# A hybrid decoder trunk on one core: the experts' weight pipeline is recut

## The reference

```python
def swiglu(h, w_gate_up, w_down):
    g, u = jnp.split(h @ w_gate_up, 2, axis=-1)
    return (jax.nn.silu(g) * u) @ w_down

def moe_ffn(h, router, w_gate_up, w_down):
    ...
    top_v, top_i = lax.top_k(logits, TOP_K)            # 2 of 8
    gates = jax.nn.softmax(top_v, axis=-1)
    combine = jnp.sum(jax.nn.one_hot(top_i, N_EXPERTS) * gates[..., None], axis=1)
    for e in range(N_EXPERTS):
        out = out + combine[:, e:e + 1] * swiglu(t, w_gate_up[e], w_down[e])
```

## Time and profile before

| | |
|---|---|
| median of 3 runs | 1663.63 us (1662.83 to 1664.7) |
| span of the profiled execution | 1657.2 us |
| PE busy | 1585.0 us, 96% |
| DVE busy | 1014.2 us, 61% |
| ACT busy | 913.3 us, 55% |
| POOL busy | 971.8 us, 59% |
| read from HBM | 428.91 MB |

### The profile page before, as it was taken

The page is one execution under the profiler, slowest core; times in us unless marked ns, Lnnn a source line. Parts: engine busy times, 40 slices in busy tenths (PEclk is TensorE's granted clock), DMA queues, the critical chain, the costliest instruction groups (busy, mean ns, idle before and its releaser), DMA issues.

```text
span 1657.2 us, 22184 instructions
## 1 busy us (share of the span) xinstructions
PE 1585.0 (96%) x6965; PEld 1232.3 (74%) x6965; DVE 1014.2 (61%) x951; ACT 913.3 (55%) x904; POOL 971.8 (59%) x457
## 2 busy tenths in 40 slices
PE   7997899999888789999999999999999999999998
PEld 4666478888755656887887888888888788888886
DVE  2103344444324336778778777877877877877875
ACT  2202244443315214776776776776776776776774
POOL 1100134445211012996996896897897797797795
PEclk9997999999988888999999999999999999999999
DMA  6342255554233044999999999999999999999993
GB/s 218 114 150 79 97 187 198 177 194 161 95 132 102 0 153 159 366 367 314 364 356 323 366 367 312 365 367 312 365 364 315 364 366 312 366 366 320 358 365 139
DMA packets 322107, 430.67 MB, mean 260 GB/s; under 512 B 13878, under 2 KB 282235, under 8 KB 322044
## 3 DMA queue, kind: packets, MB, share of 16 engines
q1 hardware_dynamic: 322044, 430.01, 76.0%
HBM read 428.91 MB, written 1.05 MB: 259 GB/s over the span
## 4 chain that ended last, share of the span: by engine, by line
PE 45%; POOL 35%; issue 14%; DVE 2%; ACT 2%; POOLq 1%; DMA 1%; DVEq 0%; SPq 0%; ACTq 0%
POOL wlo L532 34%; PE PS L1012 9%; PE PS L1014 9%; PE PS L1013 9%; PE PS L863 7%; PE PS L905 3%; PE PS L831 2%; PE PS L942 2%; PE PS L1124 1%; POOLq L529 1%; PE PS L874 1%; ACT xn L666 0%; PE PS L932 0%; POOL rstd L500 0%; PE PS L1149 0%
## 5 line engine op out<-in xcount | busy, mean ns | idle before, releaser
L532 POOL TENSOR_TENSOR wlo<-ring,whi 128x384 fp32r<-128x384 f32 x378 | 945.2, 2515 | 399.5 <-ACT whi L612 394.0
L1298 DVE TENSOR_TENSOR wlo<-ring,whi 128x1664 fp32r<-128x1664 f32 x378 | 767.8, 2034 | 269.3 <-ACT whi L612 268.6
L612 ACT ACTIVATE whi<-ring 128x2048 fp32r<-128x2048 f32 x378 | 723.5, 1915 | 136.3 <-PE PS L1014 109.8
L1012 PE MATMUL PS<-whi,xhi 128*128 128x512 f32 x1120 | 449.8, 402 | 5.1 <-DVE xlo L1645 2.4
L1014 PE MATMUL PS<-whi,xlo 128*128 128x512 f32 x1120 | 438.2, 391 | 0.0
L1013 PE MATMUL PS<-wlo,xhi 128*128 128x512 f32 x1120 | 437.6, 391 | 0.0
L1012 PEld LDWEIGHTS PS<-whi,xhi 128*128 128x128 f32 x1120 | 211.0, 188 | 52.9 <-POOL wlo L532 8.9
L1014 PEld LDWEIGHTS PS<-whi,xlo 128*128 128x128 f32 x1120 | 210.7, 188 | 45.3
L1013 PEld LDWEIGHTS PS<-wlo,xhi 128*128 128x128 f32 x1120 | 211.5, 189 | 40.3
L1012 PE MATMUL PS<-whi,hhi 128*128 128x512 f32 x560 | 223.8, 400 | 1.5 <-DVE hlo L1325 1.5
L1014 PE MATMUL PS<-whi,hlo 128*128 128x512 f32 x560 | 218.7, 391 | 0.0
(11 more groups left out here) (242 smaller groups left out, 952.4 us busy)
## 6 DMA issues: line engine op xcount, KB each, us to landing
ring<-in_moe_w_gate_up SPq DMA_DIRECT2D x448, 512.0 KB, 5.3
ring<-in_moe_w_down SPq DMA_DIRECT2D x224, 512.0 KB, 5.0
ring<-in_dense_w_gate_up SPq DMA_DIRECT2D x56, 512.0 KB, 4.6
ring<-in_dense_w_down SPq DMA_DIRECT2D x28, 512.0 KB, 4.3
ring<-in_a_w_in SPq DMA_DIRECT2D x6, 1536.0 KB, 6.6
ring<-in_mem_w_kv SPq DMA_DIRECT2D x2, 2048.0 KB, 10.8
ring<-in_a_w_out SPq DMA_DIRECT2D x2, 2048.0 KB, 7.8
ring<-in_b_w_out SPq DMA_DIRECT2D x2, 2048.0 KB, 8.0
```

Of the source, the lines that this page charges most:

```text
L532: pool.tensor_tensor(wlo[:, n % CUTS, m:SLOT], ring[:, h * SLOT + m:(h + 1) * SLOT], whi[:, n % CUTS, m:SLOT].bitcast(F32), ALU.subtract). ...
L612: nc.scalar.activation(whi[:, n % CUTS, :], ring[:, h * SLOT:(h + 1) * SLOT], ACT.Copy).then_inc(S("highs"), 1)
L1012: mm(out_, lhsT=xh, rhs=wh, start=first, stop=False)
L1298: v.tensor_tensor(wlo[:, n % CUTS, 0:m], ring[:, h * SLOT:h * SLOT + m], whi[:, n % CUTS, 0:m].bitcast(F32), ALU.subtract).then_inc(S("low ...
```

## The change

The experts get their own code; the dense layer keeps the old blocks.

- **Blocks of 512.** An expert has 7 blocks (`NBE`) of 512 hidden columns. A block is six items: four gate-up items of two 128-row groups each (512 gate and 512 up columns, pieces of 2 KB), and two down items. There are still 42 items of 1 MB in an expert, with the same products, and the same six slots and three buffers. Gate and up halves now have a PSUM bank each. All seven blocks are written out; only the loop over experts remains.
- **No drain between experts.** The down items of an expert's last block come inside the first block of the next expert. Those of the last expert stand alone at the end.
- **Combine.** Its first half is issued after the gate-up items of the second block, its second half after those of the third; expert 0 has none, and the zeros are gone. The gathering of the next tokens is in the sixth block.
- **Lower halves.** DVE subtracts all 2048 columns, in the dense layer too. POOL does none.
- **Order in an item.** The eight products with `whi` come first, and wait only for ACT's part; the four with `wlo` come last.

The core of the diff, new code only, in the order of the engines:

```diff
+def expert_item(i, b, q):
+    return 6 * b + q - (0 if b == 0 and isinstance(i, int) else 2)
...
+def expert_parts(gu, dn, b, q):
+    if q < 4:
+        return [(cols(gu, g * FF + b * EB, g * FF + (b + 1) * EB)[:, 2 * q:2 * q + 2, :], slice(0, 2),
+                 slice(g * EB, (g + 1) * EB)) for g in range(2)]
...
 # ScalarE
+def expert_hi(i, b, q):
+    m, h, j = expert_slot(i, b, q)
+    if m >= CUTS or not isinstance(i, int):
+        act.wait_ge(S("through"), upto(i, PERE, NS + m - CUTS + 1))
+    act.wait_ge(S(f"slot_full{h}"), ...)
+    nc.scalar.activation(whi[:, j, :], ring[...], ACT.Copy).then_inc(S("highs"), 1)
+def expert(i):
+    first = isinstance(i, int)
+    for b in range(NBE):
+        if b == 0 and not first:
+            expert_hi(i, 0, 0)
+            expert_hi(i, 0, 1)
+        if b > 0 or not first:
+            expert_hi(i, b, 2)
+            hidden_high(i * NBE + (NB + b))
+        expert_hi(i, b, 3)
+        if b > 0 or not first:
+            expert_hi(i, b, 4)
+            expert_hi(i, b, 5)
+        if b == 1 and not first:
+            y_high()
+        act.wait_ge(S("through"), upto(i, PERE, NS + expert_item(i, b, 3) + 1))
+        nc.scalar.activation(silE, PS[0:CAP, 0, :], ACT.Silu).then_inc(S("silu"), 1)
+        if b < NBE - 1:
+            expert_hi(i, b + 1, 0)
+            expert_hi(i, b + 1, 1)
+    x_high(i + 1)
...
 # TensorE
+def expert_cut(i, b, q, j, parts):
+    pe.wait_ge(S("highs"), upto(i, PERE, PER + m + 1))
+    for out_, xh, xl, c0, first, end in parts:
+        mm(out_, lhsT=xh, rhs=whi[:, j, c0:c0 + HD], start=first, stop=False)
+        mm(out_, lhsT=xl, rhs=whi[:, j, c0:c0 + HD], start=False, stop=False)
+    pe.wait_ge(S("lows"), upto(i, PERE, PER + m + 1))
+    for out_, xh, xl, c0, first, end in parts:
+        last = mm(out_, lhsT=xh, rhs=wlo[:, j, c0:c0 + HD], start=False, stop=end)
+    last.then_inc(S("through"), 1)
+def expert(i):
+    first = isinstance(i, int)
+    pe.wait_ge(S("xlo_ready"), i + 1)
+    for b in range(NBE):
+        expert_gate_up(i, b)
+        if not first and b == 1:
+            combine(0, 6, i)          # waits for y_low and G_ready
+        if not first and b == 2:
+            pe.wait_ge(S("added0"), i)
+            combine(1, 6, i)
+        if b == 4:
+            turn_gates()
+        if b == 5:
+            pe.wait_ge(S("dispatch"), i + 2)
+            ...
+            gather()
+        if b > 0:
+            pe.wait_ge(S("h_low"), i * NBE + (NB + b))
+            expert_down(i, b, b - 1)
+        elif not first:
+            pe.wait_ge(S("h_low"), i * NBE + NB)
+            expert_down(i, 0, NBE - 1)
+        turn_expert(i * NBE + (NB + b + 1))
...
 # VectorE, within expert(i), block b
+    if b > 0 or not first:
+        expert_lo(i, b, 4)
+        expert_lo(i, b, 5)
+    if b == 1 and not first:
+        y_low(i)
+    dve.wait_ge(S("silu"), i * NBE + (NB + b + 1))
+    v.tensor_tensor(hnE, PS[0:CAP, 1, :], silE, ALU.mult).then_inc(S("h_ready"), 1)
+    if b in (1, 2) and not first:
+        add(i, f"added{b - 1}", b - 1, 6)
+    if b == 4:
+        next_dispatch(i)
+    if b < NBE - 1:
+        expert_lo(i, b + 1, 0)
+        expert_lo(i, b + 1, 1)
+ ...
+gathered(i + 1)
```

More of the change, by code:

```diff
@@ L95, in build @@
     assert NB % 2 == 0 and PER % SLOTS == 0 and PER % CUTS == 0 and len(FFN) == PER
+    EB = 4 * P
+    NBE = FF // EB
+    PERE = 6 * NBE
+    assert PERE == PER and PERE % SLOTS == 0 and PERE % CUTS == 0
+    def expert_item(i, b, q):
[4 more added lines that the diff above has]
+                     slice(g * EB, (g + 1) * EB)) for g in range(2)]
+        f = 4 * b + 2 * (q - 4)
+        return [(rows(dn)[:, f + kk:f + kk + 1, :], slice(kk, kk + 1), slice(0, D)) for kk in range(2)]
     def gu_item(b):
@@ L446, in _ @@
                     fill_big(place[n], view)
[L448 to L458, removed]
@@ L461, in _ @@
[L461 to L469, removed]
@@ L612, in hi_of, with block @@
                 nc.scalar.activation(whi[:, n % CUTS, :], ring[:, h * SLOT:(h + 1) * SLOT], ACT.Copy).then_inc(S("highs"), 1)
-            def block(i, b, nt, r=None):
+            def block(b, r=None):
                 for n in cut_item(b):
[L617 to L626, removed]
+                    if b > 0:
+                        hi_of(n, r)
+                act.wait_ge(S("through"), count(r, 3, FFN0 + gu_item(b) + 2))
+                for t in range(NT):
+                    last = nc.scalar.activation(sil[:, t], PS[:, t, 0:FB], ACT.Silu, scale=rx[:, t:t + 1])
@@ L1239, in _ @@
                 expert(i)
-            pe.wait_ge(S("xlo_ready"), passes * NE + 1)
-            combine(passes * NE)
+            pe.wait_ge(S("h_low"), passes * (NE * NBE) + NB)
+            for q in (4, 5):
+                m = q - 6
+                j, M = m % CUTS, passes * (NE * PERE) + (PER + m + 1)
+                pe.wait_ge(S("highs"), M)
+                pe.wait_ge(S("lows"), M)
+                for kk in range(2):
+                    for hh in range(2):
+                        c, c0 = 2 * (q - 4) + kk, kk * D + hh * HD
+                        last = three(PS[0:CAP, 4 + hh, :], hhiE[:, c, :], hloE[:, c, :], whi[:, j, c0:c0 + HD], wlo[:, j, c0:c0 + HD],
+                                     False, c == 3)
+                last.then_inc(S("through"), 1)
+            pe.wait_ge(S("silu"), passes * (NE * NBE) + NB)
+            for t, bank in enumerate((6, 0)):
+                combine(t, bank, passes * NE)
         @block.vector
@@ new lines, in dense, with expert_lo @@
+            def dense():
+                for b in (0, 1):
+                    block(b)
+                with dve.Fori(0, len(REST)) as r:
+                    for b in (2, 3):
+                        block(b, r)
+                for b in (NB - 2, NB - 1):
+                    block(b)
+            def expert_lo(i, b, q):
+                m, h, j = expert_slot(i, b, q)
+                dve.wait_ge(S("highs"), upto(i, PERE, PER + m + 1))
+                v.tensor_tensor(wlo[:, j, :], ring[:, h * SLOT:(h + 1) * SLOT], whi[:, j, :].bitcast(F32),
+                                ALU.subtract).then_inc(S("lows"), 1)
```

424 lines of the change are left out of this document (211 added, 213 removed).

## The result

| | median of the runs, us | lowest to highest | runs |
|---|---|---|---|
| before | 1663.22 | 1661.42 to 1664.7 | 5 |
| changed | 1673.14 | 1668.75 to 1677.0 | 5 |

The changed kernel takes 1.0066 times the time of before, interval 1.0049 to 1.0084: slower, by 9.9 us of the median. That is less than 1%, and the interval lies clear of 1. The forecast was 1679, 15.3 us more on the span. Every run's time is its span plus 1.7 to 2.1 us; the profiled execution took 1673.83 us for a span of 1672.0.

What follows compares the result with a forecast made beforehand. TensorE's own products were taken to set the pace. Experts 1 to 7 +5.0, clock +7.7, expert 0 -0.75, end +3.3 +1.0, start -0.9: span +15.3 to 1672.5, plus 6.4 makes 1679; own range 1667 to 1687, overall 1650 to 1690.

Steps and rivals of the forecast that it cites:

- The combine's wait: Second block of experts 1 to 7: TensorE waits for y_low, 3.02 us, 3.05 with restart; bounds 2.5 and 3.5.
- The removed stalls: TensorE in each expert: all 2.33 us of stalls go, giving 124.3 us per expert.
- The clock: After each combine stall, often some 3 us at half clock: 1.1 us per stall, 7.7 us in all.
- The start: Ahead of the first gather: the four zeroing products go, so it starts 0.9 us earlier.
- The end: Last two down items stand alone behind the last transposes: TensorE waits, +3.3 us, plus 1.0 us of clock.
- Expert 0: First expert: loses its stalls (-1.75) and empty combine (-1.95), gains waits around its first SiLU (+2.95): -0.75 us.
- Span to median: Whole run: the median 1663.63 us lies 6.4 above the page's span, so 6.4 us was added to the forecast span.
- The combine wasn't hidden: Rival at the combine: stalls go and y_low is ready when TensorE comes, 29 us less, 1650 us; chance 14%.
- It did not cancel: Rival on the total: stall without clock loss and slightly larger removed stalls cancel, 1665 us; chance 10%.
- TensorE waited for no loop's code: Rival at the expert loop's head: ScalarE's or VectorE's longer loop pauses, 3.2 us more per expert, 1701 us; chance 8%.
- The rival's own model, SyncE's pause: SyncE's 5.3 us gap after branching back to its expert loop's head, taken as what ScalarE's or VectorE's loop might pay.

Runs made afterwards that it cites:

- early-output: Changed kernel with y_high moved right behind the third item's cut and y_low behind the hidden lower half, in the second block; 1648.09 us, ratio 0.992.
- half the bytes: Kernel before, loading only half of each weight item for experts 1 to 7; 1663.55 us, ratio 1.0002.
- the kernel with GpSimd's share back: Changed kernel with output early and end and expert 0 mended, but GpSimd subtracting 384 of 2048 columns in the experts; 1645.9 us, ratio 0.9896.
- VectorE alone: Kernel before with all 2048 columns of every lower half on VectorE, GpSimd's share and its waits gone; 1652.17 us, ratio 0.9935.

## Why the prediction was right, and where it was off

The mechanism was right, and so was the size of its main term: the combine lost its cover, seven times, behind the chain cut, lower half, y_low. The early-output experiment takes away just that and turns 0.7% slower into 0.8% faster. The total was forecast half too high, 15.3 us where 9.9 were measured. Term by term, on the span:

- **The combine's wait**, forecast 3.02 us and 3.05 with the restart, measured 2.98, and 3.06 with the restart by the early-output kernel's expert. VectorE's 2048 columns, forecast 2.3, take 2.29.
- **The removed stalls**, forecast 2.33 us per expert, measured 2.71. Most of the other 0.38 is the pitch in the experts: I took the gain there at 0, with 0.4 us as its upper bound. Between products without a wait the mean distance went from 0.2280 to 0.2274 us, 0.3 us over an expert's some 500 products. Freer transfers, the condition that I set for it, don't look like the cause: with half the bytes an expert kept its 126.68 us. An expert without the wait takes 123.91, not 124.3. Together the wait and the stalls make +1.9 us where I had +5.0.
- **The clock, the term that was mis-sized most**: forecast 7 x 1.1 = 7.7 us, measured 2 x 1.64 = 3.3. I took the share of idles followed by the lower clock from places among light work (six of seven); among the experts' dense products it is two of seven. The price of one, forecast 1.5, was close. With the two terms above this makes experts 1 to 7 +5.2 us where I had +12.7. The first profile's two falls were met again in the two later ones; what decides which idles are followed stays open.
- **The start**, forecast -0.9 us, measured +1.3. TensorE does reach the gather 0.84 us sooner (8.67 us from 622.88 to 631.55, against 9.51 from 617.94 to 627.45). But I costed the zeroing products only as work, and they had also been cover: without them TensorE idles for 2.66 us, the low clock goes on, and the gather takes 2.10 us more. So the sign of this term was wrong.
- **The end**, forecast +3.3 and 1.0: the idle is 2.85 us, and from the final combine's first product to the end it is 8.03 us against 6.83, +1.2 from the clock. VectorE's order is what ends the idle:

```profile
1652.93 0.60 ACT L641 ACTIVATE hhi<-PS 128x512 fp32r<-128x512 f32 x1 [0.76 <-PE PS L856]
...
1650.41 4.49 DVE L1748 TENSOR_TENSOR wlo<-ring,whi 128x2048 fp32r<-128x2048 f32 x2
1654.82 0.68 DVE L1405 TENSOR_TENSOR hlo<-PS,hhi 128x512 fp32r<-128x512 f32 x1
...
1655.75 0.47 PE L1037 MATMUL PS<-whi,hhi 128*128 128x512 f32 x1 [2.85 <-DVE hlo L1405]
```

 The hidden rows are cut at 1653.5, but their subtraction stands behind both lower halves.
- **Expert 0**, forecast -0.75 us. From the dense layer's first transposes of hidden values to the end the two profiles differ by 1444.3 - 1434.4 = 9.9 us (they start at 227.7 and 222.8); less 5.2, 1.3 and 4.1 this leaves -0.7. That is what is left over, not a measurement of its parts.
- **Span to median.** I added 6.4 us to come from a span to a median. But a run's time is its span plus about 1.8. The profiled run of before was simply some 4.6 us quicker than its median (1657.2 + 1.8 = 1659.0), and that of the changed kernel was not: it comes to the dense layer's first product at 213.25 us, the profile of before at 208.49. The ten profiles of the experiments, two of the old order among them, come to it between 210.3 and 214.2, so this is the one quick profile, and not the change. So the profiles differ by 14.8 us and the medians by 9.9. That the forecast span, 1672.5, is within 0.5 us of the profiled 1672.0 is luck: the sum has 5.4 us too much, and the profile of before happened to be that much ahead.

The forecast of 1679 came out 5.9 us too high: 7.5 us too much for experts 1 to 7, 2.2 too little for the start, 0.2 too much at the end, and 0.4 in the median of before. No rival came true. The combine wasn't hidden. It did not cancel, though for that rival the smaller clock loss and the larger removed stalls both spoke. And TensorE waited for no loop's code: the experts on ScalarE and VectorE pass the seam of their loops without a gap on TensorE (123.83 us, all busy, in the early-output kernel). The Trainium skill (Runtime: NRT & Kernel Launch, Instruction fetch mechanics) has a taken branch wait for a fetch when its target lies outside the window of two pages; for these two loops the trace shows nothing of the kind on the path. The rival's own model, SyncE's pause, turned out to be no fixed price of a long loop. It stands behind all six branches back in the kernel before (5.1 to 5.3 us, 338 recorded instructions in the loop) and with half the bytes (3.0 to 3.5 us, 338). In the changed kernel it is 0.2 to 0.3 us (296 instructions), but also in the kernel with GpSimd's share back (338). What makes it, these runs don't show.

## What to carry to other kernels

In a software pipeline, an operation that another engine waits for (here y_high and y_low) belongs where its input is ready, not behind the work that was queued before it in the text; list for each such operation what stands ahead of it on its engine and what the waiter has left to do meanwhile. Here moving these two gave 25 us. What an edit is worth depends on the slack around it: VectorE alone gave 10.6 us in the old order and nothing in the new. Before you delete useless work on the bounding engine, ask whether it covered an idle and what clock the work after it will get.

## What was not expected of the hardware

- Idles of 2.81 us between dense products are followed by the lower clock in the second and fifth place in three profiles out of three, for 3.41 us, 1.64 us of loss each; idles of 1.61 us in none of seven.
- The same 32 small products of the gather take 4.17 or 6.27 us. The longer time comes with an idle of TensorE of 2.66 us ahead of them, in nine profiles of nine; the shorter in the three without it.
- SyncE's branch back to the head of its loop of 338 instructions is followed by a pause of 5.1 to 5.3 us in the kernel before and of 0.2 to 0.3 us in the kernel with GpSimd's share back.
- Whoever of GpSimd and VectorE comes second seems to wait for the first. Beside a running subtraction of VectorE GpSimd's 384 columns take 2.73 us; where GpSimd starts first they take 1.01 us, and VectorE's next 1664 columns 2.48 us in place of 1.89 (in the kernel with the share back):

```profile
797.87 2.73 POOL L570 TENSOR_TENSOR wlo<-ring,whi 128x384 fp32r<-128x384 f32 x1
...
809.66 1.01 POOL L570 TENSOR_TENSOR wlo<-ring,whi 128x384 fp32r<-128x384 f32 x1 [0.48 <-ACT whi L663]
...
809.94 2.48 DVE L1433 TENSOR_TENSOR wlo<-ring,whi 128x1664 fp32r<-128x1664 f32 x1
```

- Moving ScalarE's cuts into an idle in front of its first SiLU put the table load of 1.28 us on the path.
